# Recurrence stage: the levels' blocks turned by four 128x128 transposes in place of sixteen 64x64 products, with new places and orders

## What is computed

```python
y = rwkv7_scan(rh, heads(decay, RWKV_HEADS), kh, vh, -kk, kk * lrh)

def step(state, inp):
    r_t, w_t, k_t, v_t, a_t, b_t = inp
    sa = jnp.einsum('bhvk,bhk->bhv', state, a_t)
    state = (state * w_t[:, :, None, :] + sa[..., None] * b_t[:, :, None, :]
             + v_t[..., None] * k_t[:, :, None, :])
    return state, jnp.einsum('bhvk,bhk->bhv', state, r_t)
y = head_group_norm(y, a_lnx_g[i], a_lnx_b[i])
```

## Time and profile before

| | us |
|---|---|
| median of three runs | 1088.08 |
| lowest and highest of them | 1087.13, 1091.59 |
| the profiled execution | 1086.01 |
| its span, first to last instruction | 1084.2 |
| TensorE busy | 1037.8 (96%) |
| VectorE busy | 740.6 (68%) |
| ScalarE busy | 553.7 (51%) |
| TensorE's granted clock, mean | 0.986 |

### The profile page before, as it was taken

How to read it: one execution, slowest core, us unless ns; L and a number is a source line. 1 busy time by engine, 2 the same in 40 slices (tenths; PEclk the granted TensorE clock), 3 DMA queues, 4 the chain that set the end, 5 groups by cost and what they waited for, 6 DMA issues and landing times.

```text
span 1084.2 us, 23734 instructions
## 1 busy us (share of the span) xinstructions
PE 1037.8 (96%) x10388; PEld 986.5 (91%) x10388; DVE 740.6 (68%) x1216; ACT 553.7 (51%) x836; POOL 0.9 (0%) x7
## 2 busy tenths in 40 slices
PE   7999999899999999999798999999999999999996
PEld 6888889899999998886678999999998799999996
DVE  4799758799976667888456555566757755566554
ACT  5426354666556458755135444444667655444531
POOL 0000000000000000000000000000000000000000
PEclk8999999999999999999999999999999999999998
DMA  9958455466645653331004555456323445554451
GB/s 370 382 191 310 177 207 194 156 234 233 233 141 185 221 224 117 118 117 44 5 2 156 195 194 190 139 165 211 129 77 115 183 152 187 184 181 154 168 177 40
DMA packets 30664, 185.88 MB, mean 171 GB/s; under 512 B 3408, under 2 KB 4704, under 8 KB 13408
## 3 DMA queue, kind: packets, MB, share of 16 engines
q1 hardware_dynamic: 30560, 184.36, 47.1%
HBM read 183.29 MB, written 1.05 MB: 170 GB/s over the span
## 4 chain that ended last, share of the span: by engine, by line
PE 88%; DVE 6%; ACT 3%; DMA 1%; issue 1%; SPq 0%; DVEq 0%; ACTq 0%
PE banks L359 47%; PE banks L1338 17%; PE banks L339 5%; PE banks L356 2%; DVE wlo L319 1%; PE banks L630 1%; ACT whi L304 1%; PE banks L633 1%; DMA raw<-in_ada 1%; PE banks L568 1%; PE banks L1860 1%; PE banks L1877 1%; PE banks L1870 1%; PE banks L1522 1%; DVE adac L552 1%
## 5 line engine op out<-in xcount | busy, mean ns | idle before, releaser
L319 DVE TENSOR_TENSOR wlo<-raw,whi 128x2048 fp32r<-128x2048 f32 (+3 forms) x163 | 323.1, 1983 | 173.6 <-ACT whi L304 172.8
L304 ACT ACTIVATE whi<-raw 128x2048 fp32r<-128x2048 f32 (+3 forms) x163 | 270.7, 1662 | 121.6 <-PE banks L1338 76.8
L359 PE MATMUL banks<-h_hi,whi 128*128 128x256 f32 x1376 | 182.7, 284 | 1.3 <-ACT h_hi L980 1.2
L359 PE MATMUL banks<-h_lo,whi 128*128 128x256 f32 x1376 | 178.5, 281 | 0.7 <-DVE h_lo L1052 0.7
L359 PE MATMUL banks<-h_hi,wlo 128*128 128x256 f32 x1376 | 178.3, 281 | 0.0
L359 PEld LDWEIGHTS banks<-h_hi,whi 128*128 128x128 f32 x1376 | 170.4, 190 | 5.1 <-issue 2.8
L359 PEld LDWEIGHTS banks<-h_lo,whi 128*128 128x128 f32 x1376 | 167.2, 187 | 3.5 <-issue 1.8
L359 PEld LDWEIGHTS banks<-h_hi,wlo 128*128 128x128 f32 x1376 | 168.5, 189 | 1.5 <-issue 1.0
L1364 ACT ACTIVATE u<-u 128x256 f32<-128x256 f32 x44 | 18.4, 418 | 128.9 <-DVE u L1418 128.8
L1338 PE MATMUL banks<-m_lo,whi 128*128 128x256 f32 x528 | 75.0, 280 | 0.0
L1338 PE MATMUL banks<-m_hi,whi 128*128 128x256 f32 x528 | 74.9, 280 | 0.0
(11 more groups left out here) (448 smaller groups left out, 1394.0 us busy)
## 6 DMA issues: line engine op xcount, KB each, us to landing
raw<-in_ada SPq DMA_DIRECT2D x24, 1024.0 KB, 5.3
raw<-in_w_up SPq DMA_DIRECT2D x22, 1024.0 KB, 4.8
raw<-in_a_gu SPq DMA_DIRECT2D x22, 1024.0 KB, 4.8
raw<-in_b_gu SPq DMA_DIRECT2D x22, 1024.0 KB, 4.8
raw<-in_w_in SPq DMA_DIRECT2D x12, 1024.0 KB, 6.1
raw<-in_w_down SPq DMA_DIRECT2D x16, 704.0 KB, 4.1
raw<-in_a_in SPq DMA_DIRECT2D x11, 1024.0 KB, 5.6
raw<-in_a_down SPq DMA_DIRECT2D x16, 704.0 KB, 4.1
```

The costliest lines, as they stand in the source:

```text
L304: act.activation(hi_s[k % NSPLIT][:, 0:w], raw[n % NRAW][:, 0:w], ACT.Copy).then_inc(*hi_made.tick(k))
L319: dve.tensor_tensor(lo_s[s][:, 0:w], raw[n % NRAW][:, 0:w], hi_s[s][:, 0:w].bitcast(F), SUB).then_inc(*lo_made.tick(k))
L359: i_ = pe.matmul(b[0:m, j * T:(j + 1) * T], a[:, kt * step + j * m:kt * step + j * m + m], x[:, kt, :], start=st, stop=sp)
```

## The change

A turn becomes four transposes of 128x128, each over two neighbouring columns of blocks (`D[:, 2n:2n+2, :]`), with the 128x128 identity, all into the group's one bank B0. So block (j, h, ti, par), which stood in column 4h + 2j + ti on half par, stands turned in column 4h + 2j + par on half ti. To match, step a writes its product into half ti of the bank of par, and step b reads half ti and writes half par of the bank of ti, both in the order of `by_tiles`. ScalarE copies one bank, and VectorE adds with D's columns taken ti first.

```diff
+        def in_turn(b):
+            return b.rearrange("p (a t) f -> p t a f", t=2)
-        def away(h, par):
-            return HALF[par if h == 0 else 1 - par]
+        def turned(j, h, par):
+            return 4 * h + 2 * j + par
+
+        def by_tiles():
+            for j in range(2):
+                for h in range(2):
+                    for ti in range(2):
+                        for par in range(2):
+                            yield j, ti, h, par
...
-                for j, ti, h, par in every():
-                    x = pe.matmul((B0, B2)[h][away(h, par), col(2 * j + ti)], D[HALF[par], blk(j, h, ti), :],
-                                  C("id64")[HALF[par], :], start=True, stop=True)
+                for n in range(4):
+                    x = pe.transpose(B0[:, n * P:n * P + P], D[:, 2 * n:2 * n + 2, :].rearrange("p t f -> p (t f)"),
+                                     C("ident"))
...
-                for j, ti, h, par in every():
+                for j, ti, h, par in by_tiles():
                     n = blk(j, h, ti)
-                    x = pe.matmul((A0, A2)[h][away(h, par), col(2 * j + ti)], A1[HALF[par], n, :], D[HALF[par], n, :],
+                    x = pe.matmul((A0, A2)[par][HALF[ti], col(2 * h + j)], A1[HALF[par], n, :], D[HALF[par], n, :],
                                   start=True, stop=True)
...
-                for j, ti, h, par in every():
-                    n = blk(j, h, ti)
-                    x = pe.matmul((B0, B2)[h][HALF[par], col(2 * j + ti)], E[away(h, par), n, :], X[away(h, par), n, :],
-                                  start=True, stop=True)
+                for j, ti, h, par in by_tiles():
+                    x = pe.matmul((B0, B2)[ti][HALF[par], col(2 * h + j)], E[HALF[ti], turned(j, h, par), :],
+                                  X[HALF[ti], 4 * par + 2 * h + j, :], start=True, stop=True)
...
-                act.activation(eight(blocks(k)), halves_of(B), ACT.Copy).then_inc(*bk_a.tick((q, s)))
+                act.activation(blocks(k), v8(B[:, 0:512]), ACT.Copy).then_inc(*bk_a.tick((q, s)))
...
-                dve.tensor_tensor(eight(D), halves_of(B), eight(D), ADD).then_inc(*bk_v.tick((q, s)))
+                dve.tensor_tensor(in_turn(D), halves_of(B), in_turn(D), ADD).then_inc(*bk_v.tick((q, s)))
```

More of the change, by code:

```diff
@@ L2199, in pe_a @@
             back(0, "TA", "TB")
-            run(7, 1)
+            run(6, 1)
             back(0, "GA", "GB")
@@ L2280, in pe_a @@
             back(1, "N1")
-            back(2, "C2")
-            back(1, "gate")
-            back(2, "C3", "gate", "N0", "N1")
+            back(2, "C2", "C3", "gate", "N0", "N1")
+            out(0, 1)
             out(2, 1)
             out(0, 2)
-            out(2, 1)
-            out(0, 2)
-            out(2, 2)
-            out(1, 4)
+            out(1, 2)
+            out(0, 1)
+            out(1, 2)
+            out(2, 3)
         def act_a(act):
@@ L2487, in dve_a @@
             mem(2, "normed")
+            front(0, "at")
             mem(3, "normed")
             scale(5)
-            front(0, "kn", "rk", "kt")
+            split(7)
             shift(5)
-            front(0, "bt", "at")
-            split(7)
-            front(0, "rt")
             split(8)
-            back(0, "GA", "GB", "GC")
             front(1, "lg")
+            back(0, "GA", "GB")
             scale(6)
-            back(0, "D")
+            back(0, "GC", "D")
             split(9)
@@ L2502, in dve_a @@
             shift(6)
+            scale(7)
             back(0, "b0")
+            split(10)
+            back(0, "a1")
             front(1, "k0")
-            back(0, "a1")
+            shift(7)
+            back(0, "b1")
+            scale(8)
             front(2, "lg")
-            scale(7)
-            back(0, "b1")
-            split(10)
             back(0, "a2")
-            shift(7)
+            split(11)
+            shift(8)
             back(0, "b2")
-            scale(8)
+            scale(9)
@@ L2514, in dve_a @@
             back(0, "a3")
-            split(11)
+            split(12)
             back(0, "b3")
-            shift(8)
-            front(1, "kn", "rk")
+            front(1, "kn")
+            front(0, "bonus")
+            shift(9)
+            front(1, "bt")
             back(0, "a4")
-            front(1, "bt", "at")
+            front(1, "at")
+            front(2, "k0")
+            front(1, "rk")
             back(0, "b4")
-            front(1, "kt")
-            scale(9)
-            front(1, "rt")
+            front(1, "kt", "rt", "bonus")
@@ L2525, in dve_a @@
+            front(2, "kn")
             back(0, "G")
-            shift(9)
-            split(12)
-            front(2, "k0")
+            front(2, "rk")
+            scale(10)
+            front(2, "rt", "kt")
             back(0, "X3", "X4")
-            front(2, "kn", "rk", "kt")
-            back(0, "C1")
-            scale(10)
-            front(0, "bonus")
-            back(0, "C2")
             shift(10)
             front(2, "bt")
-            front(1, "bonus")
-            front(2, "at", "rt")
+            back(0, "C1")
@@ L2539, in dve_a @@
+            front(2, "at", "bonus")
+            back(0, "C2")
+            split(13)
+            back(1, "GA", "D")
             back(0, "N0")
-            back(1, "GA")
-            front(2, "bonus")
-            back(1, "D", "GC")
+            back(1, "GB", "GC", "a0")
             back(0, "N1")
-            split(13)
-            back(1, "GB", "a0")
-            back(2, "GA", "D")
-            back(1, "b0")
-            back(2, "GB", "GC")
-            back(1, "a1")
+            back(1, "b0", "a1")
@@ L2550, in dve_a @@
+            back(2, "GA")
+            back(1, "b1")
+            back(2, "GB", "D", "GC")
+            back(1, "a2")
             back(2, "a0")
-            back(1, "b1")
+            back(1, "b2")
             back(2, "b0")
-            back(1, "a2")
+            back(1, "a3")
             back(2, "a1")
-            back(1, "b2")
+            back(1, "b3")
             back(2, "b1")
-            back(1, "a3")
+            back(1, "a4")
             back(2, "a2")
-            back(1, "b3")
+            back(1, "b4")
@@ L2560, in dve_a @@
             back(2, "b2")
-            back(1, "a4")
+            back(1, "G")
             back(2, "a3")
-            back(1, "b4", "G")
+            back(1, "X4")
             back(2, "b3")
@@ L2566, in dve_a @@
             back(2, "a4")
-            back(1, "X4")
+            back(1, "C1")
             back(2, "b4")
-            back(1, "C1")
-            back(2, "G")
             back(1, "C2")
-            back(2, "X4", "X3")
+            back(2, "G", "X3", "X4")
             back(1, "N0")
```

222 lines of the change are left out of this document (112 added, 110 removed).

## The result

| | before | after |
|---|---|---|
| median, us (20 runs each, same chip) | 1088.53 | 1085.6 |
| ratio of the times, 95% interval | | 0.9971 (0.9961 to 0.998) |
| span of the profiled execution | 1084.2 | 1086.4 |
| TensorE's instructions (products, and as many weight loads) | 10388 | 9968 |
| start of the input projection, us | 387.60 | 390.11 |

0.29% less, some 3 us: inside what the forecast called no change, 1 us from the predicted median, and clear of the noise, since the interval leaves out 1. The profiled execution took 1088.19 us, and its input projection begins 2.5 us later than before, though not one line ahead of it differs; over all traces of this case that start lies between 386.2 and 392.6 us. So places in the stage are given from its first product.

The account below looks back on a forecast made before the run. Instruction supply, some 73 per us, was taken to limit groups 1 and 2, where TensorE has 9.3 us idle. Gains of 0.8 and 0.7 us, with group 0's +1.4 inside, gave -1.5 us: 1086.6 us, range 1081.5 to 1091.

Parts of the forecast that it names:

- what the forecast called no change: Whole kernel: a time within about 0.5% (5.4 us) of the kernel before, given a chance of 0.76.
- predicted median: Whole kernel: median of the runs after the change, 1086.6 us, from 1088.08 us less 1.5 us.

Follow-up runs that it names:

- e11: Kernel before with only the new turn (old order of calls), plus 14 one-column products ahead of each turn of groups 1 and 2: 1092.37 us, ratio 1.0035.
- e7: Kernel before, plus 12 one-column products ahead of each of group 0's five turns, among the input projection's products: 1097.37 us, ratio 1.0087.
- e2: Kernel before with only the new turn and its places, in the old order of calls on all engines: 1083.34 us, ratio 0.9966.
- e5: Kernel before, plus 12 one-column products ahead of each turn of groups 1 and 2: 1095.75 us, ratio 1.0071.
- e8: Kernel before with the new turn in the old order of calls, but the turns of groups 1 and 2 side by side: 1084.54 us, ratio 0.9968.
- e10: Kernel before with the new turn, the new order of calls up to X3 of group 0 and the old order behind it: 1086.71 us, ratio 0.9986.
- e4: Changed kernel with each transpose issued twice into the same place: 1089.49 us, ratio 1.0016 to the kernel before.

## What to carry over

Count matrix instructions from the x of a row, and for each operation from its own row: transposes and float32 products differ by a factor of two. Where a stage of small products is neither full nor waiting for a semaphore, count its instructions per microsecond, and look for idle time that ends behind the start of an instruction block; this stage took 73 per us, and a turn in fewer instructions gained 4.5 us in the median, where TensorE's own time for it went from 0.52 us to 0.41 among filler and to 0.58 in the late levels. And when a step is moved back on one engine, look for all that wait for it, not for the one that you want sooner.

## What the runs showed of the hardware

- A 128x128 transpose of float32 is one matrix instruction and one weight load, 0.109 us; a 64x64 float32 product is two and two, 0.033 us for a product in a row of them. A 64x64 product of one column takes 0.03 us too (12 in 0.37 us): one column in place of 64 saves nothing.
- In the dense stretch, 515 to 550 us, instruction blocks of 16 KB came no closer than 3.2 us (e11), in the mean of a trace 3.7 to 4.0 us apart, some 250 TensorE records each; and in all 68 stalls TensorE went on 2.2 to 2.9 us behind the start of a block.
- An instruction block seldom starts while a 1 MB weight chunk lands: 5 of 312 did, more than half a microsecond before its end. With many small products at a chunk's end there were stalls of 1.3 to 2.8 us, one of 1.34 us even in the stage that takes 42 instructions per us on average (e7).
- Behind issue stalls of 1.3 to 2.8 us the granted clock was at 1.2 GHz for 3.4 to 10.2 us (e2, e5, e7, e8, e10, e11). Stalls of 1.2 and 1.4 us in the kernel before and one of 1.4 us in e8, late in the stage, had no such stretch behind them, nor had the wait of 1.6 us in the changed kernel, while the same wait in e4 had. What decides between them these runs do not show.
